# One step less of pipeline between the softmax and the value products of an attention loop

## The reference

```python
# A) sparse attention, 8 heads of 64: each query keeps its top 128 admissible keys
logits = jnp.einsum('bqhd,bqkhd->bhqk', qb, kg) * (HEAD_DIM ** -0.5)
logits = jnp.where(valid[:, None], logits, -jnp.inf)
p = jax.nn.softmax(logits, axis=-1)
y_attn = jnp.einsum('bhqk,bqkhd->bqhd', p, vg)
# C) attention into 256 memory tokens, 4 heads of 64
logits = jnp.einsum('bshd,bmhd->bhsm', mq, mk) * (HEAD_DIM ** -0.5)
y_mem = jnp.einsum('bhsm,bmhd->bshd', jax.nn.softmax(logits, axis=-1), mv)
# and then
x = x + jnp.concatenate([y_attn, y_pool, y_mem], axis=-1) @ w_out[l]
```

## Time and profile before

| | |
|---|---|
| median of 3 runs | 2014.12 us (2013.38 to 2014.33) |
| the profiled execution | 2014.04 us, its span 2012.2 us |
| TensorE busy | 1970.1 us, 98% of the span |
| VectorE, ScalarE, GpSimd busy | 755.7, 788.7, 891.2 us |
| attention loop | about 541 to 610 us and 1538 to 1608 us of the span |
| mean granted TensorE clock | 0.985 of full speed |

### The profile page before, as it was taken

One profiled execution on the slowest core, in us unless ns is written; L12 is line 12 of the kernel. 1 busy time (PEld: TensorE's weight loads), 2 busy tenths in 40 slices (PEclk: granted clock), 3 DMA queues, 4 the chain that ended last, 5 costly groups with the idle time before them and its releaser, 6 DMA issues.

```text
span 2012.2 us, 27490 instructions
## 1 busy us (share of the span) xinstructions
PE 1970.1 (98%) x9256; PEld 1586.8 (79%) x9256; DVE 755.7 (38%) x1180; ACT 788.7 (39%) x1064; POOL 891.2 (44%) x404
## 2 busy tenths in 40 slices
PE   6999999999999999999989999999999999999999
PEld 5888888777768788888878888887767678888887
DVE  5333310476662533330063333005855634333201
ACT  5434421442473444431153443225325635444311
POOL 4444444433553544444354444444336345444442
PEclk9999999989999999999999999999899999999999
DMA  5222232312112223222223222233120123322333
GB/s 177 95 94 95 94 104 94 122 64 84 42 44 74 94 95 103 94 94 95 93 85 98 100 94 94 98 101 112 64 84 32 44 80 105 98 94 94 100 98 105
DMA packets 50566, 182.54 MB, mean 91 GB/s; under 512 B 5752, under 2 KB 6008, under 8 KB 50240
## 3 DMA queue, kind: packets, MB, share of 16 engines
q1 hardware_dynamic: 49824, 178.84, 27.0%
q10 hardware_dynamic: 672, 2.80, 0.4%
HBM read 179.52 MB, written 2.10 MB: 90 GB/s over the span
## 4 chain that ended last, share of the span: by engine, by line
PE 93%; DVE 4%; issue 1%; ACT 1%; DMA 0%; DVEq 0%; ACTq 0%; SPq 0%
PE bank L447 91%; DVE sq L1115 2%; PE bank L790 1%; DVE h_lo L1109 1%; DVE sq L1117 1%; DMA x<-x_t 0%; ACT h_hi L875 0%; ACT sq L883 0%; ACT t L1048 0%; DVE x L1132 0%; DVE pt L334 0%; DVE t L1304 0%; ACT prob L1048 0%; DVEq L1109 0%; DVE z L1258 0%
## 5 line engine op out<-in xcount | busy, mean ns | idle before, releaser
L383 POOL TENSOR_TENSOR w_lo<-raw,w_hi 128x1024 fp32r<-128x1024 f32 x328 | 823.9, 2514 | 1080.4 <-ACT w_hi L903 1079.9
L903 ACT ACTIVATE w_hi<-raw 128x1024 fp32r<-128x1024 f32 x329 | 348.5, 1060 | 874.5 <-PE bank L447 874.0
L447 PE MATMUL bank<-h_hi,w_hi 128*128 128x512 f32 x1664 | 657.9, 395 | 12.1 <-ACT h_hi L875 12.1
L447 PE MATMUL bank<-h_hi,w_lo 128*128 128x512 f32 x1664 | 650.6, 391 | 0.0
L447 PE MATMUL bank<-h_lo,w_hi 128*128 128x512 f32 x1664 | 634.7, 390 | 0.0
L447 PEld LDWEIGHTS bank<-h_hi,w_hi 128*128 128x128 f32 x1664 | 314.5, 189 | 94.0 <-issue 15.8
L447 PEld LDWEIGHTS bank<-h_lo,w_hi 128*128 128x128 f32 x1664 | 313.8, 189 | 67.0 <-issue 2.3
L447 PEld LDWEIGHTS bank<-h_hi,w_lo 128*128 128x128 f32 x1664 | 314.5, 189 | 65.7
L447 PE MATMUL bank<-a_hi,w_hi 128*128 (+2 forms) x864 | 334.1, 387 | 0.0
L447 PE MATMUL bank<-a_lo,w_hi 128*128 (+2 forms) x864 | 332.8, 385 | 0.0
L447 PE MATMUL bank<-a_hi,w_lo 128*128 (+2 forms) x864 | 332.7, 385 | 0.0
(11 more groups left out here) (137 smaller groups left out, 1296.2 us busy)
## 6 DMA issues: line engine op xcount, KB each, us to landing
raw<-weights SPq DMA_DIRECT2D x332, 512.0 KB, 3.3
x<-x_t SPq DMA_DIRECT2D x4, 512.0 KB, 7.1
mem<-mem_t ACTq DMA_DIRECT2D x2, 1024.0 KB, 5.0
out_t<-x SPq DMA_DIRECT2D x8, 256.0 KB, 2.2
const<-consts SPq DMA_DIRECT2D x1, 505.5 KB, 9.8
spread_in<-spreads ACTq DMA_DIRECT2D x2, 216.0 KB
wpool<-pool_w ACTq DMA_DIRECT2D x2, 128.0 KB, 5.1
par<-params SPq DMA_DIRECT2D x1, 38.0 KB, 1.9
```

The source lines that it names most:

```text
L383: G.tensor_tensor(out=w_lo[:, s], in0=raw[:, s], in1=w_hi[:, s].bitcast(f32), op=ALU.subtract).then_inc(w_ready, 1)
L447: return nc.tensor.matmul(out_, lhsT, rhs, start=start, stop=stop, skip_group_check=True)
L903: nc.scalar.activation(w_hi[:, s], raw[:, s], ACT.Copy).then_inc(w_hi_done, 1)
```

## The change

In TensorE's loop the step of the attention is put in another order. The transposes of units n-4 and n-3 come first, then the logits of n and n+1 with the small work that followed them (`spread_rms`, `spread_sums`), then `fill`, and last the value products, now of n-4 and n-3, the units that were transposed in this same step, where they were of n-6 and n-5. The fills move so that bank 0 comes at step 48 with bank 1, where it was at 46. VectorE's, ScalarE's and GpSimd's programs stay as they are, and so do all buffers.

```diff
-FILL = {UNITS - 2: (0,), UNITS: (1,), UNITS + 2: (4,), UNITS + LAG: (2, 3)}
+FILL = {UNITS: (0, 1), UNITS + 2: (4,), UNITS + LAG: (2, 3)}
...
                     if n in POOL_UNITS:
                         pool_map(POOL_UNITS.index(n))
+                    if 0 <= n - LAG < UNITS:
+                        transpose_p(n - LAG)
+                        transpose_p(n - LAG + 1)
                     if n < UNITS:
                         logits(n)
                     for k in (NORM_EARLY + n, NORM_EARLY + n + 1):
...
                     if n - 2 in group_after:
                         spread_sums(group_after[n - 2])
-                    if 0 <= n - LAG < UNITS:
-                        transpose_p(n - LAG)
-                        transpose_p(n - LAG + 1)
-                    if 0 <= n - LAG - 2 < UNITS:
-                        times_v(n - LAG - 2)
                     for b in FILL.get(n, ()):
                         fill(b)
+                    if 0 <= n - LAG < UNITS:
+                        times_v(n - LAG)
```

## The result

| | |
|---|---|
| after, median of 4 runs | 2105.65 us (2099.65 to 2107.28) |
| before, median of 4 runs | 2014.22 us (2013.38 to 2014.52) |
| ratio | 1.0449, 95% interval 1.0437 to 1.0462 |
| the profiled execution after | 2099.65 us, its span 2097.8 us; mean granted clock 0.967 |

The forecast of 2121 us was 15 too high, inside its range and nearer than rival 1 (2081.5) or rival 2 (2148.5). The profiled execution was the fastest of the four, 85.6 us over the one of before.

The account below looks back on a forecast made before the run. TensorE, busy 98% of the span and 93% of the chain, was taken as the bound. The profiled 2014.0 plus 67.5 net waits plus 40 for the clock gave 2121.5, say 2121 us, range 2072 to 2152.

Parts of the forecast that it names:

- rival 1: Attention loops: the waits come but the clock stays high, 2081.5 us; chance 0.24.
- rival 2: Attention loops: the waits come and the clock stays low throughout, 2148.5 us; chance 0.13.
- The mechanism: Attention loop: after the logits, value products wait for mask n, mask n+1 and VectorE's copy, 2.33 us per 512-key step.
- The waits' sum: TensorE's new idle time in the attention loops: 35.7 us per layer, 71.3 in two layers.
- clock's term: Attention loops: idling lowers TensorE's clock, adding 40 us, between bounds of 0 and 67.
- the share of 0.6: Part of the clock's 67 us upper bound taken for both loops, giving +40 us; called the weakest number.
- What went away: Attention loops: TensorE's old waits for transposes' bank copies and inverse sums go, giving back 3.8 us.
- The fills: End of the attention loop: the same fill work in another place, worth nothing.
- Rival 3: Attention loops: old stalls go and no new one comes, so faster, 2010 us; chance 0.02.

Follow-up runs that it names:

- copy between the masks: The changed kernel with VectorE's copy listed between mask n and mask n+1 instead of behind both; 2060.5 us, ratio 1.0241.
- order of TensorE alone: The kernel before with transposes moved ahead of the logits, value products still of units n-6 and n-5; 2040.85 us, ratio 1.0137.
- copy ahead of the masks: The changed kernel with VectorE's copy of unit n-3 listed ahead of masks n and n+1 from step 8 on; 2038.67 us, ratio 1.0126.
- both orders turned: The kernel before, products still of n-6, from step 8 on with transposes ahead of logits and VectorE's copy ahead of its masks; 2011.34 us, ratio 0.9985.

## Why the prediction was right, and where its sizes were off

**The mechanism held.** The wait is where it was put, behind two masks in VectorE's list, and moving the copy past one or both of them shortened it by what they take. The forecast named 40 waits, 2.3 us early and 1.1 to 1.5 late; there are 41, of 2.2 us early and mostly 1.1 to 1.8 late, shorter where `spread_sums` covers them, and the longest, 2.55, at step 18, with a `split_y` between the masks. Steps 48 and 50 have none, as the fills were to see to, and step 46, for which 0.36 was left, has none either, its `spread_sums` being slow at the lower clock (1.74 us in the first layer, where 1.02 was counted). The products of steps 46, 48 and 50:

```profile
641.93 0.39 PE L447 MATMUL bank<-pt,v 128*64 128x128 f32 x4
...
645.60 0.66 PE L447 MATMUL bank<-pt,mv 128*64 128x128 f32 x8
...
648.94 0.66 PE L447 MATMUL bank<-pt,mv 128*64 128x128 f32 x8
```

**The waits' sum** was put at 71.3 us and came to 61.3. Three things account for it. The profile counts idle time from the modelled end of a matmul, some 0.08 us after the pace would have it (553.29 + 0.90 against 556.51 - 2.24 = 554.27), which is 3 us in 41 waits: a difference of counting. `split_y` was priced at its mean of 1.29 us; in the changed kernel no such instruction took more than:

```profile
L1332 DVE TENSOR_TENSOR a_lo<-yt,a_hi x16: 419/557/693, 575.1 to 1694.4; 128x512 fp32r<-128x512 f32 x8, 128x256 fp32r<-128x256 f32 x8
```

That is 0.69, the plain pace, for which the prediction had named the lower end: 5.0 us less in two layers. The mean of four in the earlier trace rows was carried by a slow one:

```profile
578.22 2.80 DVE L1332 TENSOR_TENSOR a_lo<-yt,a_hi 128x512 fp32r<-128x512 f32 x1 [0.32 <-ACT a_hi L1064]
```

The second loop of the kernel before, which the prediction did not read for this, had a mean of 0.83. The plain pace was not a given either: with the copy between the masks the mean was 1.12 in each loop. And `spread_sums` at the lower clock covers more, about 2 us, which was counted in the clock's term.

**The clock's term** was put at 40 us, of bounds 0 to 67, and came to 28. The 28 is what is left when the waits are taken off the profiled run's loss; TensorE's busy time, which grew by 28.3 us, says the same. At the median of the four runs it is 34. That the clock would fall was the right reading of the earlier trace rows; the share of 0.6 was too high, 28/67 = 0.42 of the bound (0.5 at the median). So the total came within 22 us of the profiled run with two terms too high, the waits by 10 and the clock by 12. The experiments also show that a straight share is the wrong form. For the kernels without repeated work, in their profiled executions, in us:

| kernel | idle in the loops | low level in and around the loops | lost beyond the idle time |
|---|---|---|---|
| before | 3.8 | 10 | 0 (the base) |
| order of TensorE alone | 20.8 | 31 | 9 |
| copy ahead of the masks | 22.8 | 24 | 5 |
| copy between the masks | 42.3 | 17 | 3 |
| changed | 61.3 | 99 | 28 |

The last column is the run's time less 2014.0 - 3.8 and less its idle time. By the medians it is 10, 6, 8 and 34. So with 21 to 42 us of idle time the clock cost 3 to 10 us, in no order of the idle time, and at 61 it cost 28 to 34. It is also not the same in each execution. The granted clock of the changed kernel's four runs was 0.967, 0.962, 0.961, 0.963, for 2099.65, 2105.62, 2107.28 and 2105.68 us; of the kernel with the copy between the masks 0.985, 0.975, 0.980 and 0.980, for 2055.47, 2066.81, 2060.39 and 2060.60 us. About 1.2 us go with each 0.001.

Of the two rules of the Trainium skill in the prediction ("TensorE: Matmul & The Clock Gate"), the one on short idles, "A second HAM failure mode: psum-queue depth-cycling", agrees with this trace: no gap in the loop is over 2.55 us, and the clock goes up and down between its levels, 99 of 232 us at the low one. The abstract rule of the Trainium skill on the same page, in "HAM oscillation", by which only longer gaps matter, would have given rival 1's 2081.5 us and does not hold here.

**What went away** did: 3.8 us of old stalls, seen by their absence. **The fills** were worth nothing, measured by themselves at 0.9999.

**Rival 3**, faster, needed VectorE to copy ahead of its masks. With that edit from step 8 on the shorter pipeline still loses 25 us: 8.9 are waits at steps 4 and 6, which kept the old order, and 7.1 are waits for ScalarE's copy, which is late next. I had called ScalarE's copy early in any case, which was true only as long as VectorE's was later.

**Open** is what exactly in a step makes the clock fall. The idle time alone doesn't set it: the kernel with TensorE's order alone idled 20.8 us and the one with the copy between the masks 42.3, and the low level held longer in the first (31 against 17 us, profiled executions). The mean granted clocks of their four runs overlap (0.981 to 0.982, and 0.975 to 0.985). Also open is the 0.15% of the kernel with both orders turned. And no run takes out the step with the transposes left behind the logits, so what the lost step costs under TensorE's old order is not measured.

## What to carry to other kernels

Before a stage of a pipeline is taken out, write down what each engine's list has ahead of the hand-over: an in-order engine that must first do work which needs this step's matmuls makes the hand-over wait for all of it, here mostly 1.1 to 2.5 us per step. The distance of a step was what hid that order; where the distance is to go, the producer's order has to be turned first. When such waits add idle time to TensorE, price its clock too: here it added half as much again to the waits, and most of it came back with a third of the idle time gone. Don't price it as a share of the idle time: here the two did not go in step.

## What the runs showed of the hardware that was not expected

- The kernel got 28 us faster by doing more: 744 repeated matmuls in TensorE's gaps brought the first loop's clock from 0.78 to 0.96.
- The clock's loss does not grow evenly with the idle time: waits of 61 us cost 28 to 34 us of it, idle time of 21 to 42 us cost 3 to 10, in no order of the idle time.
- Executions of the same kernel can differ in their granted clock: with the copy between the masks it was 0.975 to 0.985, for 2055 to 2067 us. Partly idle loops need not do this: with TensorE's order alone four runs lay within 1.3 us.
